# Recurrent mixer of a two-layer decoder step on one Trainium2 core: the second branch in front of the first gates, two chunks of the output projection round the last

## What is computed

```python
def lru_mixer(x, h0, conv_buf, w_in, conv_w, conv_b, w_a, b_a, w_i, b_i, lam, w_o):
    z = x @ w_in
    xr, g = z[..., :LRU_WIDTH], z[..., LRU_WIDTH:]
    xc, new_buf = causal_conv(xr, conv_buf, conv_w, conv_b)
    hs, hT = rglru(xc, h0, w_a, b_a, w_i, b_i, lam)
    y = (hs.astype(x.dtype) * jax.nn.gelu(g)) @ w_o
    return y, hT.astype(x.dtype), new_buf
```

## Time and profile before

| | us |
|---|---|
| median of 3 runs | 1485.36 |
| lowest, highest | 1484.62, 1487.17 |
| the profiled execution, its own time | 1482.5 |
| its span, first to last instruction | 1480.7 |
| TensorE busy | 1421.0 (96%) |
| VectorE, ScalarE, GpSimd busy | 687.7, 527.6, 234.3 |
| mean granted TensorE clock | 0.99 |

### The profile page before, as it was taken

One profiled execution on the slowest core, in us unless ns is written; L12 is line 12 of the kernel. 1 busy time (PEld: TensorE's weight loads), 2 busy tenths in 40 slices (PEclk: granted clock), 3 DMA queues, 4 the chain that ended last, 5 costly groups with the idle time before them and its releaser, 6 DMA issues.

```text
span 1480.7 us, 26917 instructions
## 1 busy us (share of the span) xinstructions
PE 1421.0 (96%) x10446; PEld 1301.1 (88%) x10446; DVE 687.7 (46%) x972; ACT 527.6 (36%) x855; POOL 234.3 (16%) x318
## 2 busy tenths in 40 slices
PE   9999999898989999999999989989899999999997
PEld 9756666566889999999999979988899999999996
DVE  4636565532385333223332677886733322233355
ACT  4135555522244222112221358872422211222224
POOL 0020000100165000000000553236600000000034
PEclk9999999999999999999999999999999999999999
DMA  7221010032213233122223123222233331223301
GB/s 209 76 73 26 21 24 21 18 100 86 66 49 86 85 96 118 57 72 85 85 94 108 33 65 94 63 73 75 58 105 86 96 97 57 85 85 96 118 1 61
DMA packets 180837, 111.15 MB, mean 75 GB/s; under 512 B 25896, under 2 KB 179069, under 8 KB 180768
## 3 DMA queue, kind: packets, MB, share of 16 engines
q1 hardware_dynamic: 180176, 109.41, 25.3%
q0 software_dynamic: 592, 0.79, 0.2%
HBM read 107.15 MB, written 3.02 MB: 74 GB/s over the span
## 4 chain that ended last, share of the span: by engine, by line
PE 82%; DVE 9%; ACT 3%; issue 2%; POOL 2%; SPq 0%; DVEq 0%; DMA 0%; ACTq 0%; POOLq 0%
PE ps L517 54%; PE ps L571 6%; PE ps L742 3%; PE ps L756 3%; DVE xT L1702 2%; DVE wl L1427 2%; PE ps L776 2%; PE ps L710 1%; DVE xl L1708 1%; PE ps L650 1%; PE ps L733 1%; ACT wh L1108 1%; PE ps L759 1%; PE ps L939 1%; PE ps L917 1%
## 5 line engine op out<-in xcount | busy, mean ns | idle before, releaser
L517 PE MATMUL ps<-xh,wl 128*128 128x280 f32 x1584 | 334.3, 292 | 0.0
L517 PE MATMUL ps<-xh,wh 128*128 128x280 f32 x1584 | 332.6, 291 | 0.9 <-DVE wl L1427 0.8
L517 PE MATMUL ps<-xl,wh 128*128 128x280 f32 x1584 | 331.2, 290 | 0.0
L517 PEld LDWEIGHTS ps<-xh,wh 128*128 128x128 f32 x1584 | 251.8, 188 | 2.0 <-issue 1.0
L517 PEld LDWEIGHTS ps<-xh,wl 128*128 128x128 f32 x1584 | 252.5, 189 | 0.0
L517 PEld LDWEIGHTS ps<-xl,wh 128*128 128x128 f32 x1584 | 249.7, 188 | 0.0
L1427 DVE TENSOR_TENSOR wl<-raw,wh 128x2048 fp32r<-128x2048 f32 (+2 forms) x79 | 196.3, 2485 | 99.6 <-ACT wh L1108 99.6
L1108 ACT ACTIVATE wh<-raw 128x2048 fp32r<-128x2048 f32 (+2 forms) x79 | 162.9, 2062 | 205.6 <-PE ps L517 191.6
L1748 DVE TENSOR_TENSOR ht<-sg,ps 128x560 f32<-128x560 f32 x44 | 32.5, 738 | 273.1 <-PE ps L517 264.1
L1928 POOL TENSOR_TENSOR acc<-xT 128x560 f32<-128x560 f32 x4 | 6.5, 1630 | 778.8 <-DVE xT L1645 669.3
L1342 ACT ACTIVATE hh<-ht 128x560 f32 (+1 forms) x44 | 29.6, 672 | 271.6 <-DVE ht L1748 271.6
(11 more groups left out here) (329 smaller groups left out, 2395.2 us busy)
## 6 DMA issues: line engine op xcount, KB each, us to landing
raw<-in_ffn_w_gu SPq DMA_DIRECT2D x176, 256.0 KB, 3.7
raw<-in_ffn_w_down SPq DMA_DIRECT2D x48, 384.0 KB, 4.3
raw<-in_lru_w_in SPq DMA_DIRECT2D x16, 512.0 KB, 4.6
Ctok<-in_cache_latent SPq DMA_DIRECT2D x48, 128.0 KB, 2.2
raw<-in_mla_w_o SPq DMA_DIRECT2D x16, 256.0 KB, 3.7
raw<-in_ffn_w_down SPq DMA_DIRECT2D x16, 256.0 KB, 5.1
raw<-in_lru_w_o SPq DMA_DIRECT2D x16, 256.0 KB, 3.3
raw<-in_mla_w_in SPq DMA_DIRECT2D x9, 256.0 KB, 5.9
```

The lines of the kernel that those rows point to most:

```text
L517: mm = pe.matmul(ps[:, 1024 * jp + 512 * h:1024 * jp + 512 * h + TH], w[:, k, col:col + P], x[:, k, h * TH:(h + 1) * TH], start=(k == 0 an ...
```

## The change

It alters the order in layer 1's mixer at both ends. At the head `opening` takes all four tiles, so that the branch of block 1 goes to pair 3 in front of the gates of block 0; these go to pairs 2 and 1, and ScalarE takes the first two GELUs in front of `xch`. At the tail `side_by_side` and `chunk` are replaced by `lru_out`, which keeps the four tiles of chunks 45 and 46 in the four pairs at once: tile 0 up to k = 3, the last gates, tile 0's k = 4 and 5, the other tiles up to k = 5, then k = 6 and 7 of all four. The split of chunk 46 moves in front of the last gates' elementwise work on ScalarE and VectorE, the transposes in front of the fourth tile of `last_chunks`, both copies to `hrow` to ScalarE inside `closing`, GpSimd's four DMAs behind `total`. `hist` lies at another address.

```diff
@@ -236,6 +236,7 @@
         put = area(reg, LIMIT)
         yh = put("yh", [P, KD, T], F32R)
         yl = put("yl", [P, KD, T], F32R)
+        hist = put("hist", [P, KD, 36])
         U = [put(f"U{s}", [P, UL]) for s in range(2)]
         gel = [put(f"gel{s}", [P, T]) for s in range(2)]
         th = [put(f"th{s}", [P, T]) for s in range(2)]
@@ -246,7 +247,6 @@
         xch = put("xch", [P, T], F32R)
...
-        hist = put("hist", [P, KD, 36])
...
@@ -519,31 +519,6 @@
-            def side_by_side(c, u, ready, done1, before=None, x=(xh, xl)):
...
-            def normed(n):
...
 
-            def last_chunks(c, us, K_, rh, rl, n):
+            def last_chunks(c, us, K_, rh, rl, n, beside=None):
 
                 pe.wait_ge(lo_ok, c + 1)
                 pe.wait_ge(f0_ok, c)
@@ -591,23 +566,26 @@
                 for t in range(4):
                     if t == 2:
                         pe.wait_ge(lo_ok, c + 2)
-                    part(us[t // 2], K_, 256, P * (t % 2), rh, rl, 0, t).then_inc(n_part, 1)
+                    part(us[t // 2], K_, 256, P * (t % 2), rh, rl, 0, t,
+                         beside if t == 3 else None).then_inc(n_part, 1)
                     if t == 0:
                         pe.wait_ge(n_acc, 5 * n + 3)
                         total(2048, 3, acc, True, True).then_inc(n_mean, 1)
                 pe.wait_ge(n_mid, n + 1)
                 for t in range(4):
+                    if t == 2 and beside is not None:
+                        pe.wait_ge(r_te, 2)
                     part(us[t // 2], K_, 256, P * (t % 2), rh, rl, 1, 4 + t).then_inc((t0_ok, t1_ok)[t % 2], 1)
                     if t == 0:
                         statistics(n, 0)
-            def opening(c, n, done1, tiles=4):
...
                 for h in range(2):
-                    for t in range(tiles):
+                    for t in range(4):
                         if h == 0 and t % 2 == 0:
                             pe.wait_ge(lo_ok, c + t // 2 + 1)
...
-            def lru_gates(j, u):
...
                 for g in range(2):
                     for n, (w, x) in enumerate(((wh[u], xch), (wh[u], xcl), (wl[u], xch))):
                         for h in range(2):
-                            at = 1024 * (2 + g) + 512 * h
+                            at = 1024 * at_pair[g] + 512 * h
                             mm = pe.matmul(ps[:, at:at + TH], w[:, W_D + g * P:W_D + (g + 1) * P],
                                            x[:, h * TH:(h + 1) * TH], start=(n == 0), stop=(n == 2))
...
             u0 = C_LRU % 2
-            opening(C_LRU, 1, r_g, 3)
+            opening(C_LRU, 1, r_g)
             pe.wait_ge(f0_ok, C_LRU + 2)
-            lru_gates(0, u0)
-            lru_branch(C_LRU + 1, 1 - u0)
+            pe.wait_ge(f1_ok, C_LRU + 1)
+            lru_gates(0, u0, (2, 1))
             with pe.Fori(0, KD // 2 - 1) as i:
                 for s in range(2):
                     c = C_LRU + 2 + s
                     lru(i * 2 + c, i * 2 + (2 + s), c % 2)
+
+            def lru_out(tile, ks):
+
+                c, jp = C_LO + tile // 2, tile % 2
+                hi, lo = (w[c % 2][:, 0:W_D].rearrange("p (k n) -> p k n", k=KD) for w in (wh, wl))
+                for k in ks:
+                    pe.wait_ge(r_yl, k + 1)
+                    for i, (w, x) in enumerate(((hi, yh), (hi, yl), (lo, yh))):
+                        for h in range(2):
+                            mm = pe.matmul(ps[:, 1024 * tile + 512 * h:1024 * tile + 512 * h + TH],
+                                           w[:, k, jp * P:jp * P + P], x[:, k, toks(h)],
+                                           start=(k == 0 and i == 0), stop=(k == KD - 1 and i == 2))
+                return mm
+
+            pe.wait_ge(lo_ok, C_LO + 1)
+            pe.wait_ge(f0_ok, C_LO)
+            lru_out(0, range(4))
             lru_gates(KD - 1, 1 - u0)
+            lru_out(0, range(4, 6))
+            pe.wait_ge(f1_ok, C_LO)
+            lru_out(1, range(6))
+            pe.wait_ge(lo_ok, C_LO + 2)
+            pe.wait_ge(r_ge, 2 * KD)
+            lru_out(2, range(6))
+            lru_out(3, range(6))
+            for tile in range(4):
+                lru_out(tile, range(6, KD)).then_inc((t0_ok, t1_ok)[tile % 2], 1)
+
             def histories(k):
 
-                if k == KD - 1:
+                if k == 0:
                     pe.wait_ge(r_hc, KD)
                     pe.wait_ge(r_hh, KD)
-                    pe.wait_ge(r_ge, 2 * KD)
                     for n in range(KD):
-                        mm = pe.transpose(ps[0:36, 2048 + n * P:2048 + (n + 1) * P], hist[:, n, :], ident[:])
+                        mm = pe.transpose(ps[0:36, 3072 + n * P:3072 + (n + 1) * P], hist[:, n, :], ident[:])
                     mm.then_inc(r_t, 1)
 
-            side_by_side(C_LO, C_LO % 2, lambda k: pe.wait_ge(r_yl, k + 1), t1_ok, histories, (yh, yl))
-            chunk(C_LO + 1, (C_LO + 1) % 2, KD, 256, yh, yl)
-            pe.wait_ge(r_te, 2)
-            last_chunks(C_LO + 2, (C_LO % 2, 1 - C_LO % 2), KD, yh, yl, 2)
+            last_chunks(C_LO + 2, (C_LO % 2, 1 - C_LO % 2), KD, yh, yl, 2, histories)
...
@@ -1275,6 +1276,11 @@
                 act.activation(spare[:], ones[:, 0, 0:1], ACT.Sqrt)
+                if n == 2:
+                    act.wait_ge(r_t, 1)
+                    for j in range(2):
+                        act.activation(hrow[:, 512 * j:512 * j + 512], ps[0:36, 3072 + 512 * j:3584 + 512 * j],
+                                       ACT.Copy).then_inc(r_te, 1)
...
                 for g in range(2):
-                    act.activation(halves(gr[u][:, g, :]), pair(2 + g), ACT.Tanh, scale=0.5,
+                    src = pair((2, 1)[g] if isinstance(j, int) and j == 0 else 2 + g)
+                    act.activation(halves(gr[u][:, g, :]), src, ACT.Tanh, scale=0.5,
                                    bias=col(hvec, KD * g, j)).then_inc(r_ge, 1)
...
@@ -1392,24 +1399,26 @@
                 if above_zero(j):
                     split_next(c, q, u, W_LRU)
                     gates(c - 1, j - 1, 1 - u)
+                first = isinstance(j, int) and j < 2
+                if first:
+                    act.wait_ge(r_g, j + 1)
+                    act.activation(halves(gel[u][:]), pair(1 + 2 * j), ACT.Gelu_apprx_tanh).then_inc(f1_ok, 1)
                 act.wait_ge(r_cv, j * 3 + 3)
                 act.wait_ge(t1_ok, c)
                 act.activation(xch[:, 0:NP], xc[u][:, 0:NP], ACT.Copy)
                 act.activation(xch[:, NP:T].rearrange("p (b s) -> p b s", b=B),
                                samples_of(xc[u]), ACT.Copy).then_inc(r_xh, 1)
-                act.wait_ge(r_g, j + 1)
-                if above_zero(j - 1):
+                if not first:
+                    act.wait_ge(r_g, j + 1)
                     act.wait_ge(r_yl, j - 1)
-                act.activation(halves(gel[u][:]), pair(1), ACT.Gelu_apprx_tanh).then_inc(f1_ok, 1)
+                    act.activation(halves(gel[u][:]), pair(1), ACT.Gelu_apprx_tanh).then_inc(f1_ok, 1)
                 if above_zero(j):
                     scale_of_input(j - 1, 1 - u)
 
             chunk_loop(act, C_LRU, KD, lru, head=2)
+            split_next(C_LO, 0, 0, 0)
             gates(C_LRU + KD - 1, KD - 1, (KD - 1 + C_LRU) % 2)
             scale_of_input(KD - 1, (KD - 1 + C_LRU) % 2)
-            split_next(C_LO, 0, 0, 0)
-            act.wait_ge(r_t, 1)
-            act.activation(hrow[:, 0:512], ps[0:36, 2048:2560], ACT.Copy).then_inc(r_te, 1)
...
@@ -1639,6 +1648,8 @@
                     src = pair(s)
                     if isinstance(c, int) and c == C_WO:
                         src = ps[:, 2048:4096].rearrange("p (h j c) -> p h j c", h=2, j=2)[:, :, s, 0:TH]
+                    if isinstance(c, int) and c == C_LO + 1:
+                        src = pair(2 + s)
...
@@ -1830,14 +1841,12 @@
 
             chunk_loop(dve, C_LRU, KD, lru, head=2)
             last = (KD - 1 + C_LRU) % 2
+            split_next(C_LO, 0, 0)
             gated(KD - 1, last)
+            outputs_lo_part(KD - 2, 1 - last)
             scaled(KD - 1, last)
-            outputs_lo_part(KD - 2, 1 - last)
             scan(KD - 1, last)
             outputs_lo_part(KD - 1, last)
-            split_next(C_LO, 0, 0)
-            dve.wait_ge(r_t, 1)
-            dve.tensor_copy(hrow[:, 512:1024], ps[0:36, 2560:3072]).then_inc(r_te, 1)
             dve.wait_ge(n_x, 2 * KD)
             for j in range(2):
                 residual(C_LO + j, j, 0, 0, True, j > 0)
...
@@ -2013,12 +2022,12 @@
             chunk_loop(pool, C_LRU, KD, lru, head=2)
             states(KD - 1, (KD - 1 + C_LRU) % 2)
             outputs_hi_part(KD - 1, (KD - 1 + C_LRU) % 2)
+            total(C_LO, 2)
             pool.wait_ge(r_te, 2)
             pool.dma_start(conv_prompt[0, 0], hrow[0:3, :]).then_inc(r_out, 16)
             pool.dma_start(conv_sample[0].rearrange("b j d -> (b j) d"), hrow[3:27, :]).then_inc(r_out, 16)
```

(1 more changed line is left out.)

21 lines of the change are left out of this document (2 added, 19 removed).

## The result

The changed kernel takes 1488.3 us (median of 18 runs, 1486.5 to 1492.3) where the kernel before takes 1484.7 in the same session (18 runs): a ratio of 1.0026, interval 1.0018 to 1.0035. It is **slower by about 4 us**. The forecast was 1482.7 and its range ended at 1486.0. The profiled execution took 1488.0 us with a span of 1486.2, 5.5 us over the span before.

A forecast was written before the change was run, and what follows sets the result against it. TensorE, busy 96% of the span, was taken to bound the kernel, so only its idle or slow time could be gained. Head -0.3, clock +2.1, tail -4.5 gave -2.7 us from 1485.4, so 1482.7; range 1480.3 to 1486.0.

The forecast's parts named there:

- The head: Layer 1 mixer's start: second branch before first gates turns a 2.1 us pause into 4.9 us, gaining 0.3 us before clock effects.
- the shift: Whole loop after the head: everything comes 1.8 us later, bounds +0.4 to +2.2.
- the clock's price: Behind the head's new pause: 15 to 24 matmuls at half rate cost 1.6 to 2.5 us, taken at 2.1.
- The loop: Between head and tail: each turn hangs on the input's end, so a delay is not caught up; period near 14.4 us.
- The tail: Output tiles round the last gates: TensorE runs without a stop, last_chunks starts at 1006.5 not 1011.02, gain 4.5 us.
- The likeliest case: The forecast itself: half rate after the head's pause, none after the tail's; -2.7 us, 1482.7; chance 0.36.
- the second case: Rival: half rate behind both the head's and the tail's pause, +2.1 us, 1484.8; chance 0.28.
- What is moved for nothing: Transposes, hrow copies and GpSimd's four output DMAs at the tail: moved at no cost; uncovered transposes would cost 1.0 us.
- The slower case: Rival: clock comes back late at the head, 108 matmuls at half rate cost 11.3 us, 1491.9; chance 0.08.
- the case that the runs before lose more than their profile: Rival: half rate behind the old 3.09 us pause costs some 1.5 us that the change removes, 1481.2; chance 0.16.
- a limit by length alone: Skill's rule for TensorE pauses: limit above 3.09 us, so head's pause punished, tail's not, 1482.7; rows were said to disagree.
- third and fourth: Rivals: no half rate at either pause (1481.3, chance 0.12); earlier runs losing more than profiled (1481.2, chance 0.16).

The follow-up runs named there:

- e11: Changed kernel with GpSimd's four output DMAs behind the bias sums and 22 unread matmuls in the head's pause: 1481.1 us, ratio 0.9985.
- e2: Changed kernel with the head put back as before: 1485.9 us, ratio 1.0013.
- e1: Changed kernel with GpSimd's four output DMAs moved behind bias(2) instead of in front: 1481.65 us, ratio 0.9986.
- e4: Kernel before with one edit, total(C_LO, 2) in front of GpSimd's four output DMAs, so these stand directly before bias(2): 1490.6 us, ratio 1.0045.
- e3: Kernel before with the head's change alone: 1486.5 us, ratio 1.0010.
- e18: Kernel before with only the bias sums of norms 0 and 2 held until VectorE's last low part: 1482.7 us, ratio 0.9991.
- e14: Changed kernel with a 128x8 memset on GpSimd between the four DMAs and bias(2): one profiled run 1485.9 us; timed again, 1482.1 us, ratio 0.9987.
- e8: Changed kernel with the four DMAs behind bias(2) and three 128x560 memsets on GpSimd in front of it: 1482.3 us, ratio 0.9988.
- e16: Whole change plus late bias sums at norms 0 and 2, 22 unread matmuls in the head's pause and 11 in the tail's: 1477.2 us, ratio 0.9953.
- e6: Changed kernel, DMAs still in front, but bias(2) waits for VectorE's last low part: 1481.3 us, ratio 0.9983.
- e12: Changed kernel with the head as before, late bias sums at norms 0 and 2, 11 unread matmuls before last_chunks: 1478.8 us, ratio 0.9969.

## Why the prediction was wrong

**The head.** Right in kind: gates without a pause, then one on `wl`, half rate behind it, and the loop passes the shift on. The gates start at 884.88 us as forecast (884.9), so the 24 matmuls of the first half did cost nothing. The pause was 5.36 us and not 4.9, for a named reason: I took 2.56 us for VectorE's subtraction, and after the change it took 2.97.
```profile
888.85 2.97 DVE L1436 TENSOR_TENSOR wl<-raw,wh 128x2304 fp32r<-128x2304 f32 x1 [2.14 <-ACT wh L1109]
```
The shift came out at 2.4 us (900.42 against 897.99 before), not 1.8. Of the 0.6 more, 0.4 is the later start of the input (891.95 for 891.5), nearly all of it this subtraction, which also swallowed the gain of 0.3 us; 0.2 is the clock's price, taken at 2.1 and measured at 2.2 against e11 and 2.3 against the kernel before (8.47 us for what took 6.17). GpSimd's sums for the norm before ran beside the subtraction in both kernels; what made it longer by 0.4 us the trace does not tell.

**The loop.** Right: the period stayed near 14.4 us and the shift was not caught up.

**The tail.** Right: no pause from the last branch to the last output tile, and e2, which has no shift, starts `last_chunks` at 1006.73 where I had 1006.5.

**The clock at the tail.** The likeliest case said full rate behind that pause; it came back at half, as in the second case. With the shift this left 0.5 us of gain at the statistics, against the 0.6 that case gives. Had nothing else moved, the result would have been about "same". e1 is that kernel: ratio 0.9986, some 2.1 us less. That this lies near the forecast's 2.7 is luck in part, since the forecast counted on full rate at the tail, and e1 has half.

**What is moved for nothing: the step that failed.** "On POOL the four output DMAs leave the place in front of `total` ... and go behind it, in front of `bias`, whose sum is read only when the hidden half is multiplied out." In the sum this stood at nothing. The reason is true, and beside the point. The sum's reader was late, but its neighbour was not: VectorE's norm steps run beside the sums and read two operands from SBUF, and TensorE's first tile waits for them group by group. With the four DMAs directly in front of the sums, every step took 0.97 us. I had looked for who reads the result, and not for who works beside it. Its price was 5.5 us in e4 and 5.9 in the changed kernel, by far the largest term. That the order does it is shown; why a sum directly behind a DMA meets VectorE so stays open. The trace of before held the hint: one step in four at 0.89 beside the sums, and the steps just ahead of them all at 0.50. The transposes, with their 1.0 us, were covered as said: from the mean (1014.16 before, 1013.69 after) to the wait for `ssq` it takes 16.3 us in both.

**The rivals.** The slower case had 0.08 and another mechanism; the clock did not come back late at the head. Of the case that the runs before lose more than their profile: half rate behind the pause of 3.09 us does happen. The timeline of e4's TensorE, at the last gates and at `last_chunks`:
```profile
980.40 0.53 PE L1042 MATMUL ps<-xch,wh 128*128 128x280 f32 x2 [3.07 <-DVE xcl L1824]
...
1011.16 0.37 PE L571 MATMUL ps<-yh,wh 128*128 128x280 f32 x1 [0.92 <-DVE xT L1643]
```
The granted clock from 980 to 990 us is 0.83 there and 1.00 before, yet `last_chunks` starts at 1011.16, only 0.14 later: the pause of 1.73 us behind it shrinks to 0.67 and swallows it. So that rival's 1.5 us do not show in this profile, nor in e3's (0.89, and 30.7 us from the last gates to `last_chunks` as before). Some executions do lose more than the profile of before, but in another place: e18, an edit of the kernel before, has the half rate at 290 to 295 us that e14 has (granted 0.53) and loses 2.8 us by 306. That this also lies behind the median of before was not profiled. Against a limit by length alone speaks also that some 3.1 us went both ways, in code that is the same up to there.

**The working.** Three slips in it bear on nothing: the third of the first case with the third and fourth is 0.40, not 0.39; the range's low end by its own words is 1480.7, not 1480.3; the clock's bounds give the forecast 1482.2 to 1483.1, not 1481.9 to 1483.5.

**VectorE beside GpSimd.** The two patterns show that VectorE and GpSimd hold each other up. The Trainium skill, SBUF — State Buffer, section Who interferes with whom, says that a VectorE instruction with two SBUF inputs contends with a GpSimd instruction that reads SBUF and not with one that only writes it. With this the traces agree: beside e8's memsets the steps take 0.50. The Trainium skill, the same page, section SBUF: two separate sides, says that whichever of the two is first holds the shared pair of ports for its whole instruction. With this they do not: a sum lasts 1.8 to 2.1 us, and a step beside it is held for 0.4, with three more running at 0.50 within the same sum.

## What to carry to other kernels

When a piece of work is moved on an engine that nobody waits for, ask not only who reads its result but which engine works beside it and may be held up; here that neighbour fed TensorE step by step. Price a pause of TensorE with the half rate behind it, and where nothing better fits in, put a few matmuls there that nobody reads, after timing one of them: e11 and e16 so kept full rate at the head, where every profile with the pause of 5.36 us open came back at half. A profile with one 0.89 among 0.50s is a hint worth a trial: late bias sums (e6, e12, e16, e18) were never slower.

## What the runs showed that I had not expected

- Two stable patterns between the same two streams: four VectorE steps per sum in 2.08 us, or two in 1.79 us. A memset of 0.12 us on GpSimd decides between them, and 6 us of the program hang on it.
- A pause of one length is followed by full rate in some executions and by half rate in others: 3.07 to 3.09 us (full before and in e18, half in e3 and e4), 2.84 us (full in e11, half in the changed kernel, e1 and e2), 2.57 to 2.60 us at 433 to 434 us (full in e1, half before).
- In the profiles of e14 and e18 2.8 us are lost between 290 and 306 us, far in front of all edits of the mixer, at a granted 0.53 from 290 to 295 us. Distances between two events within one profile are a safer reading than the ends of two profiles.
